# Expert weights of a mixture-of-experts layer read from one array in order of use, instead of from three arrays in their own order

## The chip, the cores and the metric

One core of one Trainium2 chip runs the whole program. The metric is the device time of one execution in microseconds (us). Before the change the median of three runs is 1352.35 us, with 1351.14 us the lowest and 1352.84 us the highest.

## What is computed

One layer of an encoder on 512 tokens of width 1024, all in float32. Three blocks, each followed by a residual sum and a layer norm:

```python
x = layer_norm(a * x + hybrid_mixer(x, ...))             # 8 heads of windowed attention beside a gated conv
x = layer_norm(a * x + memory_cross_attention(x, mem))   # 4 heads over 256 memory tokens
x = layer_norm(a * x + expert_choice_moe(x, ...))        # 16 experts

def expert_choice_moe(x, w_router, w_gate, w_up, w_down):
    affinity = softmax(x @ w_router)                     # (512, 16)
    gates, idx = top_k(affinity.T, 64)                   # each expert picks 64 tokens
    xe = x[idx]                                          # 16 x 64 x 1024
    hid = silu(xe @ w_gate) * (xe @ w_up)                # 16 x 64 x 2048
    ye = (hid @ w_down) * gates
    return scatter_add(idx, ye)
```

The arrays of the experts are `w_exp_gate` and `w_exp_up` (16 x 1024 x 2048) and `w_exp_down` (16 x 2048 x 1024), 8 MB for each expert and array, 384 MB together. Each weight is used once, so that each has to be read once from DRAM.

## The kernel before

**Stages.** The mixer and the cross attention fill the first 375 us. Then come the experts, two at a time: 8 pairs, the first written out and the other seven in a loop (`Fori(1, PAIRS)`) on each engine. A pair gathers the picked tokens with matmuls against a 0/1 matrix (line 929), does gate and up (line 970), turns the hidden activations (line 979), does down (line 992) and adds the result to the output tokens (matmul of line 1002, sum of line 1265). After the last pair comes the last layer norm, with the stores of the output.

**Chunks.** The weights of an expert come in 12 chunks (`CPE`) of 2 MB, those of a pair in 24 (`CPP`): for each half of the columns of gate and up, four chunks in the order gate, up, gate, up; then four of down. A chunk is [128 partitions, 4, 1024] float32 in SBUF: 16 KB in each partition, without gaps. In the chunk, partition p and index k hold the 4 KB run of row 128 (k0 + k) + p of the weight matrix. So a chunk is 512 runs of 4 KB in DRAM. For gate and up a row is 8 KB long and the run is one half of it; for down a row is 4 KB long, and the 512 runs of a chunk lie one behind the other, in an order other than that of the partitions. `exp_src(pair, j)` gives the DRAM side of chunk j, `exp_chunk(j, first)` the SBUF side.

**The ring.** SBUF has 8 slots of one chunk each. In the first pair two further chunks (8 and 9) go to other places, chunk 9 in five small transfers (line 378). All the loads are issued by SyncE (SP), in the order of use: `load_exp` has a wait of its own ahead of it, on the semaphore `exp_used`, which TensorE raises behind the last matmul of each chunk. Chunk j is issued when chunk j - 8 is used. The last chunk of each pair is loaded in two halves of 1 MB (line 335), all others in one transfer (line 338). TensorE waits in `expert_in` for the chunk's own semaphore. Nothing but the weights' loads goes through SP's queue during the experts; ScalarE's queue has small loads of the earlier stages.

**The matmuls of a chunk.** The code has 8 matmuls for a chunk, 4 k by 2 halves of the 1024 columns, each with 64 tokens loaded into the array and [128, 512] of the chunk streamed through it. In the trace they are 16 instructions in float32.

Of the kernel before, what the change touches and what calls it, by code (L numbers as in the profile page):

```python
# [1 line left out]

# [10 lines left out]
P = 128  # L36
D, S, M = 1024, 512, 256
# [6 lines left out]
E, CAP, FF = 16, 64, 2048  # L44
# [4 lines left out]
SLOT = 4096  # L49
# [4 lines left out]
CPE = 12  # L54
CPP = 2 * CPE
# [66 lines left out]


def build(nc, x, mem, w_in, na_rpb, conv_w, w_mix_out, ln1_g, ln1_b, w_mem_q, w_mem_k, w_mem_v, w_mem_out,
          ln2_g, ln2_b, w_router, w_gate, w_up, w_down, ln3_g, ln3_b, consts, out):
    with ExitStack() as ctx:
        def sb(name, *shape):
            return ctx.enter_context(nc.sbuf_tensor(name, [P, *shape], F32))
# [60 lines left out]
        gate = kv[:, 64:128].rearrange("p (i t e) -> p i t e", i=PAIRS, t=TT)  # L189
# [112 lines left out]
                return scattered[k][2][:, 512 * c:512 * c + 512] if k < 3 else scattered[3 + c][2]  # L302
            return exp_chunk(j, first)[:, k, 512 * c:512 * c + 512]

        wg_v = w_gate[0].rearrange("e (k p) f -> e p k f", p=P)
        wu_v = w_up[0].rearrange("e (k p) f -> e p k f", p=P)
        wd_v = w_down[0].rearrange("e (k p) d -> e p k d", p=P)

        def exp_src(pair, j):
            e, n = 2 * pair + j // CPE, j % CPE  # L310
            if n < 8:
                g, w, k = n // 4, (wg_v, wu_v)[n % 2], 4 * (n % 4 // 2)
                return w[bass.ds(e, 1), :, k:k + 4, 1024 * g:1024 * g + 1024].rearrange("e p k f -> (e p) k f")
            k = 4 * (n - 8)
            return wd_v[bass.ds(e, 1), :, k:k + 4, :].rearrange("e p k d -> (e p) k d")

        def key_tokens(v, a):

# [8 lines left out]
        def _(sp):  # L327
# [3 lines left out]
            def load_exp(j, pair=0, first=True):  # L331
                landed = extra_in[0] if first and j == EXTRA else exp_in[exp_slot(j, first)]
                if j == CPP - 1:
                    for h, semaphore in enumerate((half_in, landed)):
                        sp.dma_start(exp_chunk(j, first)[:, 2 * h:2 * h + 2], exp_src(pair, j)[:, 2 * h:2 * h + 2])\
                            .then_inc(semaphore, 16)
                    return
                sp.dma_start(exp_chunk(j, first), exp_src(pair, j)).then_inc(landed, 16)  # L338
# [38 lines left out]
            for row, cols, room in scattered:  # L377
                sp.dma_start(room, exp_src(0, EXTRA + 1)[:, row, cols]).then_inc(extra_in[1], 16)
# [910 lines left out]


_INS = ["x", "mem", "w_in", "na_rpb", "conv_w", "w_mix_out", "ln1_g", "ln1_b", "w_mem_q", "w_mem_k", "w_mem_v",
        "w_mem_out", "ln2_g", "ln2_b", "w_router", "w_exp_gate", "w_exp_up", "w_exp_down", "ln3_g", "ln3_b"]


# [19 lines left out]
```

## Time and profile before

| | |
|---|---|
| span of the profiled execution | 1350.2 us |
| median of three runs (no profile) | 1352.35 us |
| from the start to the first expert matmul of line 929 | 375.7 us |
| TensorE (PE) busy | 1165.1 us, 86% |
| DMA from 394 to 1321 us | 409 GB/s |
| read from DRAM | 435.50 MB |

The profiled execution has no time of its own apart from its span; the span runs from its first to its last instruction and is 2.15 us below the median of the runs (1352.35 - 1350.2), which is what lies around it. The page divides the span into 40 slices of 33.75 us each; a digit is a busy share in tenths. A DMA packet is one run of bytes that one of the 16 DMA engines moves. A mean DMA share can come out a little over 1, because an engine's packets overlap at their ends.

### The profile page before, as it was taken

Reading aid. Unit: us, or ns where it says so; the run is one execution under the profiler, and the core shown is the slowest. Engines: PE = TensorE matmul, PEld = TensorE weight load, DVE = VectorE, ACT = ScalarE, POOL = GpSimd, SP = SyncE. Lnnn points to the kernel's source line nnn. Section 1 sums busy time; section 2 is a strip of 40 time slices with the busy share of each in tenths; the row PEclk is TensorE's granted clock in tenths of the full one; section 3 lists DMA queues with packets and bytes.
Section 4 is the critical chain, followed back from the end, with each engine's and each line's share of the span. In section 5 each row is a group of like instructions: output and inputs, shape, how many; then the busy total and the mean of one; then the engine's idle time right before and its main releaser. Section 6 shows DMA issues by size and latency. Waiting matters only on the chain.

```text
span 1350.2 us, 13739 instructions
## 1 busy us (share of the span) xinstructions
PE 1165.1 (86%) x5680; PEld 591.3 (44%) x5680; DVE 291.4 (22%) x472; ACT 196.5 (15%) x366; POOL 123.0 (9%) x60
## 2 busy tenths in 40 slices
PE   7999988999599999889779978987897799789874
PEld 6786866897553343243224322422432243234221
DVE  2014587646610020020002002000200020020005
ACT  4233434043100000000000001000000000010003
POOL 3312323430003000000000000000000000000003
PEclk9999999999689999999999999999999999999997
DMA  9513112065759999999999999999999999999993
GB/s 317 129 63 125 63 63 94 0 235 233 280 196 409 409 409 410 409 409 410 410 410 410 410 409 410 409 410 410 410 410 410 410 410 410 410 410 410 410 410 121
DMA packets 123228, 438.03 MB, mean 324 GB/s; under 512 B 6575, under 2 KB 11966, under 8 KB 123198
## 3 DMA queue, kind: packets, MB, share of 16 engines
q1 hardware_dynamic: 118080, 432.09, 81.0%
q10 hardware_dynamic: 5118, 5.52, 1.6%
q8 instruction: 22, 0.36, 0.1%
q14 instruction: 8, 0.07, 0.0%
HBM read 435.50 MB, written 2.11 MB: 324 GB/s over the span
## 4 chain that ended last, share of the span: by engine, by line
PE 53%; DMA 31%; DVE 7%; SPq 3%; ACT 3%; issue 1%; POOL 1%; POOLq 0%; ACTq 0%; DVEq 0%
PE bank L970 17%; DMA ring<-in_w_exp_down 13%; DMA ring<-in_w_exp_up 11%; PE bank L992 8%; DMA ring<-in_w_exp_gate 7%; PE bank L929 5%; PE bank L1002 4%; SPq L338 3%; PE bank L693 3%; PE bank L698 3%; PE bank L695 3%; PE bank L682 2%; PE bank L674 1%; PE bank L804 1%; PE bank L806 1%
## 5 line engine op out<-in xcount | busy, mean ns | idle before, releaser
L970 PE MATMUL bank<-ring,yt 128*64 128x512 f32 x2048 | 454.6, 596 | 69.8 <-DMA ring<-in_w_exp_up 35.5
L970 PEld LDWEIGHTS bank<-ring,yt 128*64 128x64 f32 x2048 | 143.7, 137 | 363.5 <-issue 259.1
L992 PE MATMUL bank<-ring,yt 128*64 128x512 f32 x992 | 222.6, 596 | 38.1 <-DMA ring<-in_w_exp_down 25.9
L992 PEld LDWEIGHTS bank<-ring,yt 128*64 128x64 f32 x992 | 71.9, 137 | 168.9 <-issue 115.5
L1259 DVE TENSOR_TENSOR work<-bank,work 128x512 f32<-128x512 f32 x32 | 22.1, 692 | 473.9 <-PE bank L970 473.9
L641 ACT ACTIVATE work<-bank 128x512 f32<-128x512 f32 x32 | 19.1, 597 | 576.5 <-PE bank L970 576.5
L409 POOL TENSOR_SCALAR stat<-stat 128x1 f32<-128x1 f32 x3 | 1.7, 554 | 906.2 <-ACT work L659 906.2
L1265 DVE TENSOR_TENSOR xT<-bank,xT 128x512 f32<-128x512 f32 x64 | 44.3, 691 | 171.6 <-PE bank L1002 171.6
L929 PE MATMUL bank<-yt,res 128*128 128x128 f32 x512 | 63.4, 284 | 13.3 <-DVE yt L1245 13.3
L929 PEld LDWEIGHTS bank<-yt,res 128*128 128x128 f32 x512 | 60.4, 197 | 25.6 <-DVE xT L1265 17.7
L402 POOL TENSOR_TENSOR piece<-ring,piece 128x1024 fp32r<-128x1024 f32 x24 | 57.7, 2406 | 146.3 <-ACT piece L477 146.3
L1002 PE MATMUL bank<-yt 128*128 128x512 f32 x128 | 61.7, 618 | 6.0 <-ACT yt L648 6.0
L693 PE MATMUL bank<-x_hi,piece 128*128 128x512 f32 x192 | 49.2, 398 | 3.6 <-ACT piece L477 1.9
L644 ACT ACTIVATE yt<-bank 128x512 f32<-128x512 f32 x32 | 19.1, 597 | 203.8 <-PE bank L979 203.8
L695 PE MATMUL bank<-x_lo,piece 128*128 128x512 f32 x192 | 47.5, 389 | 0.0
L698 PE MATMUL bank<-x_hi,piece 128*128 128x512 f32 x192 | 47.5, 389 | 0.0
L1002 PEld LDWEIGHTS bank<-yt 128*128 128x128 f32 x128 | 19.7, 188 | 48.4 <-DVE xT L1265 31.6
L693 PEld LDWEIGHTS bank<-x_hi,piece 128*128 128x128 f32 x192 | 35.0, 188 | 11.0 <-ACT ring L503 2.2
L695 PEld LDWEIGHTS bank<-x_lo,piece 128*128 128x128 f32 x192 | 36.1, 188 | 7.6
L698 PEld LDWEIGHTS bank<-x_hi,piece 128*128 128x128 f32 x192 | 36.0, 188 | 7.5
L648 ACT ACTIVATE yt<-bank 64x512 f32<-64x512 f32 x32 | 18.9, 591 | 121.9 <-PE bank L992 121.5
L674 PE MATMUL bank<-cst,work 128*128 128x128 f32 (+1 forms) x100 | 15.4, 277 | 23.1 <-DVE work L1222 13.2
(147 smaller groups left out, 960.2 us busy)
## 6 DMA issues: line engine op xcount, KB each, us to landing
ring<-in_w_exp_gate SPq DMA_DIRECT2D x64, 2048.0 KB, 23.6
ring<-in_w_exp_up SPq DMA_DIRECT2D x64, 2048.0 KB, 23.7
ring<-in_w_exp_down SPq DMA_DIRECT2D x54, 2048.0 KB, 23.8
ring<-in_w_exp_down SPq DMA_DIRECT2D x16, 1024.0 KB, 19.9
ring<-in_w_in SPq DMA_DIRECT2D x5, 2048.0 KB, 9.0
ring<-in_w_mix_out SPq DMA_DIRECT2D x2, 2048.0 KB, 7.7
res<-in_x SPq DMA_DIRECT2D x4, 512.0 KB, 5.5
ring<-in_w_in SPq DMA_DIRECT2D x4, 512.0 KB, 9.1
```

Source lines behind the costliest of these rows:

```text
L338: sp.dma_start(exp_chunk(j, first), exp_src(pair, j)).then_inc(landed, 16)
L402: nc.gpsimd.tensor_tensor(piece[:, p % 2, 1, :, :], raw_piece(p), piece[:, p % 2, 0, :, :].bitcast(F32), ALU.subtract).then_inc(lo_split, 1)
L674: mm = nc.tensor.transpose(pt[n % 2][0:cols, a * P:a * P + rows], src, ident[0:rows, 0:rows])
L682: mm = nc.tensor.matmul(pj[n % 2][:, 0:width], lhs(c), rhs(c), start=c == 0, stop=c == k - 1)
L693: nc.tensor.matmul(pj[n % 2][:, :], hi[:, k, :], x_hi[:, k, :], start=k == 0, stop=False)
L695: nc.tensor.matmul(pj[n % 2][:, :], hi[:, k, :], x_lo[:, k, :], start=False, stop=False)
L698: mm = nc.tensor.matmul(pj[n % 2][:, :], lo[:, k, :], x_hi[:, k, :], start=False, stop=k == KT - 1)
L929: mm = nc.tensor.matmul(pv[k // 4][:, P * (k % 4):P * (k % 4) + P], res[:, t, P * k:P * k + P], pick[:, t].rearrange("p e n -> p (e n)"), ...
L970: mm = nc.tensor.matmul(bank[2 * g + n % 2][64 * c:64 * c + 64, :], xeT[:, kk, 64 * e:64 * e + 64], exp_rhs(j, first, k, c), start=kk == 0 ...
L992: mm = nc.tensor.matmul(bank[5][64 * n:64 * n + 64, :], hidT[:, s, 64 * c:64 * c + 64], exp_rhs(j, first, s, n), start=(g, c, s) == (0, 0, ...
L1002: mm = nc.tensor.matmul(pv[(c + 1) % 2][:, :], scat[:, t, :], ye[:, 512 * n:512 * n + 512], start=True, stop=True)
L1265: nc.vector.tensor_tensor(y, pv[(c + 1) % 2][:, :], y, ALU.add).then_inc(mix_kept, 1)
```

## The change

The host makes one array `w_exp` of the three, of 192 chunks x 128 partitions x 4096 floats (`SLOT`), in order of use. Partition p of a chunk is then 16 KB in one piece, and the chunk 2 MB in one piece. The DRAM side of a load is one line. SBUF side, slots, order, waits, sizes and counts of transfers, and all matmuls stay; so do the two halves of the last chunk (each partition's 8 KB are in one piece in it) and the five small transfers of chunk 9 (4 KB or 2 KB in each partition, as before).

```diff
-        wg_v = w_gate[0].rearrange("e (k p) f -> e p k f", p=P)
-        wu_v = w_up[0].rearrange("e (k p) f -> e p k f", p=P)
-        wd_v = w_down[0].rearrange("e (k p) d -> e p k d", p=P)
+        chunks = experts.rearrange("c p (k n) -> c p k n", k=4)
 
         def exp_src(pair, j):
-            e, n = 2 * pair + j // CPE, j % CPE
-            if n < 8:
-                g, w, k = n // 4, (wg_v, wu_v)[n % 2], 4 * (n % 4 // 2)
-                return w[bass.ds(e, 1), :, k:k + 4, 1024 * g:1024 * g + 1024].rearrange("e p k f -> (e p) k f")
-            k = 4 * (n - 8)
-            return wd_v[bass.ds(e, 1), :, k:k + 4, :].rearrange("e p k d -> (e p) k d")
+            return chunks[bass.ds(CPP * pair + j, 1)].rearrange("c p k n -> (c p) k n")
...
+def expert_chunks(gate, up, down):
+    out = np.empty((E, CPE, P, 4, 1024), np.float32)
+    for n in range(8):
+        w = (gate, up)[n % 2][0].reshape(E, 2, 4, P, 2, 1024)
+        out[:, n] = w[:, n % 4 // 2, :, :, n // 4].transpose(0, 2, 1, 3)
+    out[:, 8:] = down[0].reshape(E, 4, 4, P, D).transpose(0, 1, 3, 2, 4)
+    return out.reshape(E * CPE, P, SLOT)
```

## Rows read from the trace of the kernel before

**Rows 1.** The page: busy tenths of TensorE and DMA, GB/s, in 40 slices.

```profile
PE   7999988999599999889779978987897799789874
...
DMA  9513112065759999999999999999999999999993
GB/s 317 129 63 125 63 63 94 0 235 233 280 196 409 409 409 410 409 409 410 410 410 410 410 409 410 409 410 410 410 410 410 410 410 410 410 410 410 410 410 121
```

**Rows 2.** The chain that ended last, two pairs' parts: start us, us, what.

```profile
679.12 24.28 DMA ring<-in_w_exp_down
...
703.53 7.10 PE bank L992 x32
...
751.04 24.03 DMA ring<-in_w_exp_gate
...
777.03 20.48 DMA ring<-in_w_exp_up
797.51 28.76 DMA ring<-in_w_exp_down
826.41 7.10 PE bank L992 x32
```

**Rows 3.** The same view: start of the first pair and of the second.

```profile
375.71 6.76 PE bank L929 x40
...
484.87 4.73 PE bank L929 x40
```

**Rows 4.** DMA view, 394 to 1321 us: packets, queues, loads with us to landing.

```profile
DMA packets 95629, 379.45 MB, mean 409 GB/s; under 512 B 3016, under 2 KB 3016, under 8 KB 95621
q1 hardware_dynamic: 95621, 379.32, 102.5%
ring<-in_w_exp_gate SPq DMA_DIRECT2D x60, 2048.0 KB, 23.6
ring<-in_w_exp_down SPq DMA_DIRECT2D x52, 2048.0 KB, 23.8
```

**Rows 5.** Timeline, last pair: start us, us, instructions, [idle before <-releaser].

```profile
1292.24 3.65 PE L970 MATMUL bank<-ring,yt 128*64 128x512 f32 x16 [1.38 <-DMA ring<-in_w_exp_up]
1297.35 3.65 PE L970 MATMUL bank<-ring,yt 128*64 128x512 f32 x16 [1.46 <-DMA ring<-in_w_exp_gate]
1302.47 3.65 PE L970 MATMUL bank<-ring,yt 128*64 128x512 f32 x16 [1.47 <-DMA ring<-in_w_exp_up]
1307.68 3.65 PE L992 MATMUL bank<-ring,yt 128*64 128x512 f32 x16 [0.97 <-DMA ring<-in_w_exp_down]
1312.72 3.65 PE L992 MATMUL bank<-ring,yt 128*64 128x512 f32 x16 [1.38 <-DMA ring<-in_w_exp_down]
1317.92 7.09 PE L992 MATMUL bank<-ring,yt 128*64 128x512 f32 x32 [0.97 <-DMA ring<-in_w_exp_down]
```

**Rows 6.** Stretches: us, busy us by engine, granted clock, DMA share, GB/s.

```profile
80.00:83.00 3.00, 3.00 (x15) 2.49 (x14) 0.00 (x0) 0.00 (x0) 0.00 (x0) 1.00 1.05 403
303.00:308.00 5.00, 4.10 (x29) 3.63 (x27) 2.21 (x8) 3.30 (x12) 0.00 (x0) 1.00 1.02 417
344.00:348.00 4.00, 3.51 (x26) 3.40 (x25) 2.59 (x3) 1.08 (x2) 1.52 (x1) 0.73 1.03 425
600.00:1300.00 700.00, 594.43 (x2782) 223.06 (x2782) 62.95 (x91) 46.28 (x72) 0.00 (x0) 1.00 1.03 410
```

**Rows 7.** DMA view of 8 to 16 us, and of 79 to 83 us.

```profile
DMA packets 4282, 2.46 MB, mean 308 GB/s; under 512 B 78, under 2 KB 4160, under 8 KB 4282
...
DMA packets 781, 1.60 MB, mean 400 GB/s; under 512 B 0, under 2 KB 0, under 8 KB 781
```

**Rows 8.** Loads issued by SP, 394 to 1321 us: min/median/max ns, first and last start.

```profile
L338 SPq DMA_DIRECT2D ring<-in_w_exp_gate x60: 367/4700/10248, 396.0 to 1268.5; - x60
L338 SPq DMA_DIRECT2D ring<-in_w_exp_up x60: 368/4783/10250, 399.4 to 1279.0; - x60
```

**Rows 9.** The page: the instruction queue, and packets of the whole span by size.

```profile
DMA packets 123228, 438.03 MB, mean 324 GB/s; under 512 B 6575, under 2 KB 11966, under 8 KB 123198
q8 instruction: 22, 0.36, 0.1%
```

More of the change, by code:

```diff
@@ L124, in build @@
 def build(nc, x, mem, w_in, na_rpb, conv_w, w_mix_out, ln1_g, ln1_b, w_mem_q, w_mem_k, w_mem_v, w_mem_out,
-          ln2_g, ln2_b, w_router, w_gate, w_up, w_down, ln3_g, ln3_b, consts, out):
+          ln2_g, ln2_b, w_router, experts, ln3_g, ln3_b, consts, out):
     with ExitStack() as ctx:
@@ L1291 @@
 _INS = ["x", "mem", "w_in", "na_rpb", "conv_w", "w_mix_out", "ln1_g", "ln1_b", "w_mem_q", "w_mem_k", "w_mem_v",
-        "w_mem_out", "ln2_g", "ln2_b", "w_router", "w_exp_gate", "w_exp_up", "w_exp_down", "ln3_g", "ln3_b"]
+        "w_mem_out", "ln2_g", "ln2_b", "w_router", "w_exp", "ln3_g", "ln3_b"]
+def expert_chunks(gate, up, down):
[5 more added lines that the diff above has]
+    return out.reshape(E * CPE, P, SLOT)
 def kernel(**inputs):
@@ L1300 @@
     arrays, args = {}, []
+    laid = {
+        "w_exp": expert_chunks(*(np.asarray(inputs[f"w_exp_{w}"]) for w in ("gate", "up", "down"))),
+    }
     for name in _INS:
-        a = inputs[name]
+        a = laid[name] if name in laid else inputs[name]
         if name == "na_rpb":
```

## The prediction, made before the changed kernel was built or run

> **What bounds the kernel now.** I read the page's slices first. From slice 13 on (about 394 us) the DMA digit is 9 and the rate is 409 or 410 GB/s in every slice up to the last, while PE moves between 7 and 9 [rows 1]. One resource is flat at its top, the other breathes: the reader is to see in this that the transfers, and not TensorE, pace the experts. The DMA view of 394 to 1321 us says the same in one line: 379.32 MB on SP's queue, 102.5% of the 16 engines' time [rows 4]. At 2.097 MB a chunk that is 379.32 / 2.097 = 181 chunks without a gap.
>
> The chain of waits confirms it. In a pair it runs through landings of 20 to 29 us, and the same matmul group of line 992 starts at 703.53 and at 826.41 us, 122.88 us apart [rows 2]. A pair has 24 chunks, so a chunk takes 122.88 / 24 = 5.120 us. The first pair, whose chunks were there in time, took 484.87 - 375.71 = 109.16 us [rows 3]. So TensorE alone would need 13.7 us a pair less than the DMA gives it. In the timeline of the last pair TensorE starts a chunk, works 3.65 us, and idles about 1.4 us for the next one [rows 5].
>
> **The change, part by part.**
>
> *TensorE, VectorE, ScalarE, POOL.* No instruction is added, removed or moved: 0 us.
>
> *SP.* The same number of loads behind the same waits. The address of a load is worked out from one index instead of two; SP is not idle-bound here: its loads take 4.7 us in the median and 0.37 us at the least [rows 8]. An instruction that can be done in 0.37 us and takes 4.7 is held up by a full queue. Its cost does not reach the end as long as a load is issued before the engines run dry, and a load lands 23.6 us after its issue where 5.12 us would be its own share [rows 4], so at least four chunks are ahead of it. If that cover were gone, each load would cost its 0.37 us beside the 5.12, still nothing. I take 0 for SP. If packets become four times larger, SP's queue holds more bytes, its loads drop towards 0.4 us, and SP waits for a free slot instead; the landing then counts up to 8 chunks, 8 x 5.12 = 41 us. That is another place of the same wait.
>
> *First ten chunks and chunk 9's five pieces.* They land before the experts begin. The first pair ran 109.16 us without a chain piece of a DMA [rows 3], so nothing of them is on the path: 0 us.
>
> *The 181 chunks behind them.* Here every 0.1 us of a chunk counts 181 times: 18.1 us. Two things change for a chunk, the place of its bytes in DRAM and the size of a packet.
>
> The place. In the timeline TensorE starts gate and up chunks at 1292.24, 1297.35 and 1302.47 us, 5.11 and 5.12 apart, and down chunks at 1307.68, 1312.72 and 1317.92, 5.04 and 5.20 apart [rows 5]. But the two kinds lie differently: a chunk of gate or up is 512 runs of 4 KB with gaps of 4 KB, a chunk of down is already 2 MB without a gap. Had DRAM been slowed by the gaps, down would be quicker; it is not. Their time from issue to landing is equal too, 23.6 and 23.8 us [rows 4]. So what the change does to the place is worth 0 by the nearest rows. Its bounds: the third kind of layout is new in that neighbouring partitions lie 16 KB apart, and no row shows it.
>
> The size of a packet. Now 95,621 packets carry 379.32 MB, none of them over 8 KB [rows 4]; taking off the 3,016 small ones leaves 92,605 of 4,096 bytes. If there is a fixed cost for each packet beside its bytes, a 16 KB packet pays it once instead of four times. What do rows say of it? 2 KB packets ran at 403 GB/s in a stretch of 3 us, and at 400 in one of 4 us [rows 6, 7]. That is 2048 x 16 / 400 = 81.9 ns a packet and engine. 4 KB packets take 4096 x 16 / 410 = 159.8 ns in the long stretch [rows 6]. A fixed part is then 2 x 81.9 - 159.8 = 4.0 ns. A 16 KB packet would take 4 x 159.8 - 3 x 4.0 = 627 ns, 418 GB/s, and a chunk 5.02 us. In short stretches, with the queue just filled, 4 KB packets ran at 417 and 425 GB/s [rows 6], 157.2 and 154.2 ns; by these the fixed part is 6.6 or 9.6 ns and a 16 KB packet takes 609 or 588 ns, 430 or 446 GB/s.
>
> But the short stretches say more than that. The same 4 KB packets, of the same weights, run at 417 to 425 GB/s for the first 4 or 5 us and then at 409 to 410 for 900 us. The engines can therefore take a 4 KB packet faster than they do. What holds the long stretch at 410 is something that they share or that stands ahead of them, and it shows no sign of a price by the packet. Writing the packets' descriptors is not it either: from 8 to 16 us 4,282 packets, nearly all under 2 KB, went through in 8 us, 1.9 ns each, where the long stretch needs one every 10 ns [rows 7]. A limit in bytes does not see the packet's size. I take the value for a limit in bytes, 0 us for a chunk, because the long stretch itself is the row nearest to the changed kernel, and keep as ends -44 us (430 GB/s: 2.097 / 0.430 = 4.877 us instead of 5.12 for a chunk, times 181) and, the other way, the slower rival's +22 us below. The 446 GB/s would be 4.70 us a chunk and -76 us; it rests on a stretch of 4 us and is the far end.
>
> The sum against the profiled execution: span 1350.2 + 0 = 1350.2 us, and with the 2.15 us around it 1352.35. I forecast 1352 us, no change.
>
> Here a page of the skill speaks for a gain. The Trainium skill, "DMA: Bandwidth & Descriptors", section "Why small descriptors are slow (HBM only)", gives the engine a fixed cost of about 3 cycles for each packet, beside one cycle for 32 bytes. By that a 16 KB packet needs 515 cycles where four of 4 KB need 524; a chunk would fall by 1.7%, as an estimate from that page to 5.03 us, and the kernel by 16 us. The trace's 2 KB stretch agrees in size with such a cost (4.0 ns); that it is what binds the long stretch, the short stretches at 417 and 425 speak against.
>
> The same page's table "Specifications" wants at least 512 bytes in a transfer for the full line rate. By that rule 4 KB runs are well past the point from which size matters, and the change is worth nothing. No row here shows more than 8 KB from DRAM into SBUF.
>
> **The rivals.**
>
> *A. The packet has a price and it binds (faster).* For it: 2 KB packets are slower for their bytes than 4 KB ones, 400 against 410. Against it: the 417 to 425 stretches. It decides as soon as a chunk lands in less than 5.12 us, because TensorE has 13.7 us a pair to give, down to 109.16 / 24 = 4.55 us a chunk. Its time: with 4.0 ns, 5.018 us a chunk, 181 x -0.102 = -18.5 us, 1334 us; with the rate of the first 5 us kept for good (417 GB/s, 5.029 us) much the same, 1336 us; with 6.6 ns, 1308 us. I take 1332 us as its middle.
>
> *B. The new places in DRAM are read more slowly (slower).* One mechanism: all the partitions of a chunk now start 16 KB apart and each engine reads 16 KB from one place before it goes on, so that the engines read in step from places that may share a part of the memory. The place is the reading side of the 181 chunks; it decides as soon as a chunk takes more than 5.12 us, since there is no slack on the DMA side at all. Price from the nearest row that ran slower at full queue, the 2 KB stretch at 400 GB/s: 2.097 / 0.400 = 5.243 us, 181 x 0.123 = +22 us, 1374 us. For it: of the 30 packets over 8 KB in the trace 22 are instruction loads of 16 KB (0.36 MB / 22), and they took 0.1% of 16 engines' span [rows 9], 0.001 x 16 x 1350.2 / 22 = 0.98 us each, 17 GB/s for an engine instead of 25.6. Those go to another memory than SBUF; at their rate a chunk would take 7.8 us and the kernel 490 us more, which I name as the far end and do not believe. Against it: gate, up and down are two different layouts with one and the same 5.12 us.
>
> *C. The change doesn't do what it says.* The queue could still cut the 16 KB into packets of 4 KB. Then only the place changes, and the time stays at 1352 us. The changed profile would tell C from my forecast, the time would not.
>
> **How the numbers follow.** No change by a limit in bytes 0.40 and C 0.16, both 1352 us, together 0.56; A 0.34; B 0.10. About 0.2% (2.7 us) is what a measurement of this kernel can tell from no change. So faster 0.34, within 0.2% 0.56, slower 0.10. The forecast is that of the likeliest case, 1352 us. For 8 in 10 the range takes in the no-change cases and most of A, down to 1318 us, which leaves out the part of A with 6.6 ns (some 0.08), and ends at 1357 us above, which leaves out B (0.09).
>
> **What would show it.** Right: the slices keep 409 or 410 GB/s from 394 us on, the group of line 992 repeats every 122.88 us, and TensorE's idle ahead of a chunk stays near 1.4 us. That packets grew: about 23,000 of them over 8 KB in place of 92,605 of 4 KB, SP's loads near 0.4 us instead of 4.7, and landings of up to 41 us. In that case with 410 GB/s unchanged, my limit in bytes is shown. Packets grown and the rate at 418 or more is A; I would have erred in taking the short stretches for proof that the packet's cost is covered. A rate under 409 with larger packets, or with packets of 4 KB at new places, is B. Unchanged packets with unchanged time are C. What would make it wrong apart from these is a stage before 375 us that moves, and nothing of the change reaches it.

## The result, and the profile after

The changed kernel takes 1313.88 us (median of 4 runs, 1311.94 to 1314.76), the kernel before 1351.78 us beside it: a ratio of 0.9716, with a 95% interval of 0.9704 to 0.9729. That is 37.9 us less, where the forecast was no change and the range ended at 1318 us. The span of the profiled execution is 1311.9 us against 1350.2.

The page's slices for DMA and GB/s, to be read against [rows 1], and its line on packets, against the one in [rows 9] (a slice is now 32.8 us):

```profile
DMA  9513112047549999999999999999999999999992
GB/s 318 140 65 129 64 65 97 1 193 288 195 157 409 425 427 427 428 428 429 428 429 426 430 428 427 429 428 429 426 430 429 427 429 428 429 426 430 430 425 109
DMA packets 50908, 438.03 MB, mean 334 GB/s; under 512 B 6575, under 2 KB 11966, under 8 KB 25406
```

The same megabytes go in 50,908 packets instead of 123,228. 25,502 of them (50,908 - 25,406) are of 8 KB or more, where there were 30. The rate has gone from 409 or 410 to between 425 and 430 GB/s in every slice from 426 us on, nearly as flat as it was. So the packets did grow, and the rate did not stay.

SP's loads from 394 to 1285 us (min/median/max ns), against [rows 8], and the median us from issue to landing in the DMA view, against [rows 4]:

```profile
L308 SPq DMA_DIRECT2D ring<-in_w_exp x172: 327/333/348, 396.9 to 1244.3; - x172
```

```profile
ring<-in_w_exp SPq DMA_DIRECT2D x172, 2048.0 KB, 30.3
```

A load takes SP 0.33 us where it took 4.7, and lands 30 us after its issue where it took 23.6: SP is no longer held up by a full queue, and waits for free slots instead. This came as forecast, and it is not where the time comes from (see the experiment with two loads in flight, below).

The chain of waits, where [rows 2] and [rows 3] had landings at every turn (start us, us, what):

```profile
376.30 7.05 PE bank L899 x40
...
709.15 4.73 PE bank L899 x40
713.88 3.62 PE bank L940 x16
...
720.38 24.18 PE bank L940 x112
...
745.84 7.09 PE bank L962 x32
...
754.27 7.09 PE bank L962 x32
...
761.95 7.06 PE bank L940 x32
...
769.16 35.28 DMA ring<-in_w_exp
...
804.49 3.65 PE bank L962 x16
...
826.75 4.73 PE bank L899 x40
...
944.29 4.73 PE bank L899 x40
...
1061.87 4.73 PE bank L899 x40
...
1179.39 4.73 PE bank L899 x40
```

(Lines 899, 940, 962 and 972 are lines 929, 970, 992 and 1002 of the kernel before; a chunk is 16 instructions.) In the pair that starts at 709.15 us TensorE goes through 14 chunks at its own pace (16 + 112 + 32 + 32 + 32 instructions) and meets the DMA at the 15th: its timeline has the first wait for a landing before 770.23 us. The last ten chunks still come at the pace of the DMA. From 826.75 to 1179.39 us three pairs take 352.64 us, 117.55 us a pair, 4.898 us a chunk, against 122.88 and 5.120. The DMA remains the bound, with 8.4 us a pair to go to the 109.16 us of [rows 3].

The timeline of the last pair has the same step, 4.80 to 4.99 us from chunk to chunk, where [rows 5] had 5.04 to 5.21:

```profile
1245.31 3.65 PE L940 MATMUL bank<-ring,yt 128*64 128x512 f32 x16 [1.24 <-DMA ring<-in_w_exp]
1250.30 3.65 PE L940 MATMUL bank<-ring,yt 128*64 128x512 f32 x16 [1.34 <-DMA ring<-in_w_exp]
1255.10 3.65 PE L940 MATMUL bank<-ring,yt 128*64 128x512 f32 x16 [1.15 <-DMA ring<-in_w_exp]
1260.00 3.65 PE L940 MATMUL bank<-ring,yt 128*64 128x512 f32 x16 [1.25 <-DMA ring<-in_w_exp]
```

**Where the 38.3 us of the spans are.** The experts begin 0.6 us later (376.30 against 375.71). From the start of pair 0 to the start of pair 7 it is 803.1 us against 836.6 (1179.39 - 376.30; 1212.31 - 375.71), 33.5 less. The start of pair 7 in the chain of the kernel before:

```profile
1212.31 4.73 PE bank L929 x40
```

From there to the end it is 132.5 against 137.9, 5.4 less. 33.5 + 5.4 - 0.6 = 38.3. By chunks: 181 x (5.120 - 4.898) = 40.2 us. Of the 1.9 us between the two, 0.6 are the later start; the slice from 394 to 426 us, at 409 GB/s instead of 428, accounts for some 32.8 x 19 / 428 = 1.5. Why that slice is slower was not followed up.

### The profile page after: what moved, and what is told of

Same layout as the page of the kernel before. It is cut to its first block, busy times and chain, and to the rows that moved or that the text cites. A ratio compares the mean times of both kernels' runs of the same rounds, so it can differ in the third digit from the quotient of the medians.

```text
span 1311.9 us, 13711 instructions
## 1 busy us (share of the span) xinstructions
PE 1162.6 (89%) x5680; PEld 593.1 (45%) x5680; DVE 291.4 (22%) x472; ACT 196.1 (15%) x366; POOL 123.6 (9%) x60
## 2 busy tenths in 40 slices
DMA packets 50908, 438.03 MB, mean 334 GB/s; under 512 B 6575, under 2 KB 11966, under 8 KB 25406
## 4 chain that ended last, share of the span: by engine, by line
PE 71%; DMA 16%; DVE 6%; ACT 3%; issue 1%; POOL 1%; POOLq 0%; SPq 0%; DVEq 0%; ACTq 0%
PE bank L940 24%; DMA ring<-in_w_exp 16%; PE bank L962 16%; PE bank L899 5%; PE bank L972 4%; PE bank L663 3%; PE bank L668 3%; PE bank L665 3%; PE bank L652 2%; PE bank L644 1%; ACT yt L614 1%; PE bank L949 1%; PE bank L725 1%; PE bank L774 1%; PE bank L776 1%
```

## The experiments

Two theories stood after the result. **Packet**: each packet costs an engine a fixed time beside its bytes, and the four times fewer packets are the whole gain. **Place**: the bytes now lie in DRAM in the order of use, and the packets' size doesn't matter. The kernel before and the changed one give the packet theory its two numbers: 32 packets and 5.120 us, 8 packets and 4.899 us a chunk and engine, so (5.120 - 4.899) / 24 = 9.2 ns a packet and 4.825 us for the bytes. (4.899 is 117.58 / 24, the pair as the expectations took it.) All later expectations use them unchanged.

**Runs of 4 KB at the new places.** All three kernels with gaps differ from the changed one by this, with `RUN` of 1024, 2048 and 512 floats and `GAP` of 64 floats (256 bytes); the SBUF side is the same memory, viewed as runs.

```diff
-        chunks = experts.rearrange("c p (k n) -> c p k n", k=4)
+        chunks = experts.rearrange("c p (m r) -> c p m r", r=RUN + GAP)
 
         def exp_src(pair, j):
-            return chunks[bass.ds(CPP * pair + j, 1)].rearrange("c p k n -> (c p) k n")
+            return chunks[bass.ds(CPP * pair + j, 1), :, :, 0:RUN].rearrange("c p m r -> (c p) m r")
```

> The host's layout of the changed kernel, but with 256 bytes of gap behind each 4 KB run: a partition's chunk is 4 runs within 17 KB, so the places are those of the changed kernel to within 2% while a packet can't be longer than 4 KB. Theory 'packet': what counts is the number of packets. The kernel before took 122.88 / 24 = 5.120 us a chunk with 32 packets of 4 KB on each of 16 engines, the changed one 117.58 / 24 = 4.899 us with 8 packets of 16 KB; so a packet costs (5.120 - 4.899) / 24 = 9.2 ns beside its bytes and the bytes cost 4.825 us. Here: 5.120 us a chunk, 1352 us. Rival 'place': the order of the bytes in DRAM counts, packets don't: 4.90 us a chunk, 1314 us.

1353.38 us, a ratio to the kernel before of 1.0002 (0.9992 to 1.0012). Two pairs begin at

```profile
968.30 4.73 PE bank L911 x40
1091.18 4.73 PE bank L911 x40
```

122.88 us apart. That is the 122.88 us of the kernel before. With packets of 4 KB and the bytes at their new places the whole gain is gone. (The gaps make a partition's 16 KB into 17 KB, 6% and not the 2% that the expectation names.) The 4 KB runs lie 4 KB apart in gate and up before, without gaps in down before, and 256 bytes apart here; a chunk takes 5.120 us on the average of a pair in both kernels. Place falls.

**Runs of 16 KB, scattered.**

```diff
-        chunks = experts.rearrange("c p (k n) -> c p k n", k=4)
+        chunks = experts.rearrange("p (c n) -> c p n", n=SLOT + GAP)[:, :, 0:SLOT].rearrange("c p (k n) -> c p k n", k=4)
```

> The opposite: packets of 16 KB, but in DRAM each partition has a row of its own with its 192 pieces of 16 KB (256 bytes of gap behind each), so that the 128 pieces of a chunk lie 3 MB apart. Theory 'packet': 8 packets an engine, 4.90 us a chunk, 1314 us. Rival 'place': the 2 MB in one piece were what helped; scattered they take at least the 5.12 us of the kernel before, 1352 us or more.

1313.0 us, 0.9704 (0.9687 to 0.972). The stretch from 600 to 1250 us of this kernel (us, busy us by engine, granted clock, DMA share, GB/s):

```profile
600.00:1250.00 650.00, 576.47 (x2704) 216.05 (x2700) 61.63 (x90) 46.28 (x72) 0.00 (x0) 1.00 1.01 428
```

The 128 pieces of a chunk are 3 MB apart and it costs nothing. That a chunk is 2 MB in one piece has no part in the gain.

**Runs of 8 KB and of 2 KB.**

> The changed kernel with runs of 8 KB (256 bytes of gap behind each). Theory 'packet' at 9.2 ns: 4.825 + 16 x 0.0092 = 4.972 us a chunk, 181 x 0.073 = 13 us over the changed kernel, 1327 us. Rival 'place': 1314 us. A threshold between 4 and 16 KB instead of a price by the packet would give 1314 or 1352 us.

1326.2 us, 0.9808 (0.9791 to 0.9824).

```profile
950.11 4.73 PE bank L911 x40
1069.42 4.73 PE bank L911 x40
```

119.31 us a pair, 4.971 us a chunk; 4.972 was expected. There is no threshold between 4 and 16 KB.

> The changed kernel with runs of 2 KB (256 bytes of gap behind each), a long stretch of 2 KB packets, which the kernel before doesn't have. Theory 'packet' at 9.2 ns: 4.825 + 64 x 0.0092 = 5.414 us a chunk, 181 x 0.515 = 93 us over the changed kernel, 1407 us. By the rate of 400 GB/s that 2 KB packets had in a stretch of 4 us of the kernel before: 5.243 us a chunk, 1376 us. By a limit in bytes of 410 GB/s: 5.12 us, 1352 us.

1406.11 us, 1.0401 (1.0384 to 1.0419). The DMA view of this kernel from 600 to 1250 us:

```profile
DMA packets 124778, 251.46 MB, mean 387 GB/s; under 512 B 1999, under 2 KB 1999, under 8 KB 124778
```

251.46 MB in 650 us are 386.9 GB/s and 5.42 us a chunk; 5.414 was expected. This is the long stretch of 2 KB packets that the kernel before lacked: 387 GB/s, and not the 400 to 403 that the prediction read from stretches of 3 and 4 us.

**Down's weights alone.** `w_exp_down` is laid out by the host as 16 KB a partition; gate and up are read as before.

```diff
-        wd_v = w_down[0].rearrange("e (k p) d -> e p k d", p=P)
+        wd_v = w_down.rearrange("e c p (k d) -> e c p k d", k=4)
...
-            k = 4 * (n - 8)
-            return wd_v[bass.ds(e, 1), :, k:k + 4, :].rearrange("e p k d -> (e p) k d")
+            return wd_v[bass.ds(e, 1), n - 8].rearrange("e p k d -> (e p) k d")
```

> One part of the change alone: only the down weights are laid out by the host (16 KB a partition in one piece); gate and up are read as in the kernel before. A chunk of down was 2 MB without a gap before as well, so that only the packets' size and the order within the 2 MB change. Theory 'packet': 8 of 24 chunks fall from 5.120 to 4.899 us, 181 / 3 x 0.221 = 13 us: 1339 us, 121.1 us a pair. Rival 'place' as the gaps of gate and up: nothing, 1352 us.

1340.24 us, 0.9909 (0.9896 to 0.9923).

```profile
838.72 4.73 PE bank L928 x40
...
1202.17 4.73 PE bank L928 x40
```

Three pairs in 363.45 us, 121.15 a pair; (16 x 5.120 + 8 x 4.899) comes to 121.11. A chunk of down was one gapless piece of 2 MB before, so only the size of its packets and the order within the 2 MB have changed, and the kernel with scattered pieces shows that the order costs nothing. The packets' size explains this third of the gain.

**At most two loads in flight.** Ahead of each load, from chunk 12 on, SP also waits until the load two places earlier has landed. The loop over the pairs is written out on SP, so that the waits are constants; `DEPTH` is 2.

```diff
+            def landed_by(n):
+                if n >= EXTRA + EXTRAS:
+                    sp.wait_ge(exp_in[exp_slot(n % CPP, False)], 16 * ((n - EXTRA - EXTRAS) // SLOTS + 2))
...
+            for i in range(1, PAIRS):
                 for j in range(CPP):
                     sp.wait_ge(exp_used, i * CPP + (j - SLOTS + 1))
+                    landed_by(i * CPP + j - DEPTH)
                     load_exp(j, i, first=False)
```

> The kernel before, with one more wait ahead of each load of the experts from chunk 12 on: the load two places earlier has landed, so that at most two loads are in flight (4.6 on average before). SP's loop over the pairs is written out for it. It asks why 4 KB packets ran at 417 to 425 GB/s in short stretches and at 410 for 900 us. Theory 'depth': a full queue adds some 5 ns to each packet; with two in flight a chunk takes 2.097 / 0.420 = 4.99 us, 181 x 0.13 = 23 us less, 1329 us. Rival 'start-up': the short stretches are high because packets counted in them began before, or because engines are out of step only later; then depth is nothing: 5.12 us a chunk, 1352 us. If two loads are too few to keep the engines busy: over 1352 us, with gaps in the DMA's share.

1353.19 us, 1.0008 (0.9998 to 1.0018).

> The same extra wait in the changed kernel. Theory 'depth': 8 packets of 16 KB save some 5 ns each, 4.86 us instead of 4.90, 181 x 0.04 = 7 us less, 1307 us. Rival 'start-up': 1314 us.

1313.83 us, 0.972 (0.9704 to 0.9736). That there were only two in flight is seen in the DMA view of the first of the two, 600 to 1250 us, where a load lands 10.2 us after its issue, twice 5.1:

```profile
DMA packets 67077, 266.14 MB, mean 409 GB/s; under 512 B 2106, under 2 KB 2106, under 8 KB 67075
...
ring<-in_w_exp_gate SPq DMA_DIRECT2D x42, 2048.0 KB, 10.2
```

SP's loads fell to 0.37 us in it, as they did with the change, and not a us was gained. The full queue was a sign of the small packets and no cost.

**Two queues.** The odd chunks of pairs 1 to 7 are issued by GpSimd, with semaphores of their own; the first kernel has 4 KB packets (the kernel before), the second 16 KB.

```diff
-                for j in range(CPP):
+                for j in range(0, CPP, 2):
                     sp.wait_ge(exp_used, i * CPP + (j - SLOTS + 1))
                     load_exp(j, i, first=False)
...
+                    for i in range(1, PAIRS):
+                        for j in range(1, CPP, 2):
+                            pool.wait_ge(exp_used, i * CPP + (j - SLOTS + 1))
+                            landed = pool_in[exp_slot(j, False) // 2]
+                            room, src = exp_chunk(j, False), exp_src(i, j)
...
+                                nc.gpsimd.dma_start(room, src).then_inc(landed, 16)
```

> The kernel before (4 KB packets), with the odd chunks of pairs 1 to 7 issued by GpSimd instead of SP, so that each engine has two queues to take packets from. Theory 'ring': the 9.2 ns lie between two packets of one queue and the other queue's packet fills them; then a chunk falls from 5.12 towards 4.83 us and the kernel by up to 45 us, to about 1305. Theory 'engine': the price is the engine's own for each packet; 5.12 us a chunk, 1352 us. GpSimd makes its packets in software; if it makes them slower than one load in 10.2 us it becomes the bound, over 1352 us.

1355.34 us, 1.0026 (1.0017 to 1.0036). The DMA view, 600 to 1250 us:

```profile
DMA packets 67107, 266.25 MB, mean 410 GB/s; under 512 B 2107, under 2 KB 2107, under 8 KB 67107
...
q1 hardware_dynamic: 33551, 133.26, 51.4%
q0 software_dynamic: 33556, 132.99, 51.1%
```

Each queue has half of the packets and the rate is the same 410 GB/s. One queue's packets don't fill the time between the other's. (The kernel is 3.6 us slower than the one before beside it, which its rate doesn't show; where that arises was not followed up.)

This leaves one rival: the price could be charged by something that all 16 engines share. The packet records of the kept traces (start, duration and bytes of each packet) speak to that. Where at most 8 packets are under way at a time, as at the end of a load, a packet takes 84 ns at 2 KB (150 packets) and 159 ns at 4 KB (52 packets) in the kernel before, 309 ns at 8 KB (42 packets, the kernel with 8 KB runs) and 611 ns at 16 KB (6 packets, the changed kernel); all are medians. From 600 to 1250 us, with all engines at work and one size in each kernel, they take 88, 164, 314 and 613 ns. Twice a 2 KB packet less a 4 KB packet is 2 x 84 - 159 = 9 ns, and 2 x 159 - 309 is 9 ns again. So the fixed part is there while half of the engines or more stand idle: it is each engine's own.

> The same split over two queues in the changed kernel (16 KB packets). Theory 'ring': 4.83 instead of 4.90 us a chunk, 160 x 0.07 = 11 us less, 1303 us. Theory 'engine': 1314 us.

1321.17 us, 0.9775 (0.976 to 0.979), 8.6 us over the changed kernel beside it (1312.61). The rate is 428 GB/s in most of it, with dips such as 391 from 960 to 980 us; before that one TensorE waited 4.45 us for a landing inside a chunk, and the matmul that adds the results to the tokens (line 989 of this kernel) then took 9.51 us instead of 7.7, in a stretch with a granted clock of 0.74, which is partly the lower of its two levels:

```profile
920.00:940.00 20.00, 15.66 (x74) 4.96 (x70) 0.69 (x1) 1.19 (x2) 1.07 (x2) 1.00 1.01 427
940.00:960.00 20.00, 14.83 (x38) 5.69 (x39) 6.92 (x10) 2.46 (x3) 0.54 (x1) 0.74 1.01 428
960.00:980.00 20.00, 20.00 (x118) 10.38 (x118) 1.38 (x2) 0.60 (x1) 0.54 (x1) 1.00 0.97 391
```

Which of the two, TensorE's slower turn or the order in which two queues bring chunks, makes up the 8.6 us was not tried. Both theories were about the rate, and the rate says "engine".

**Packets of 32 KB.** Two neighbouring chunks in one load of 4 MB; the host puts a partition's two pieces together.

```diff
+        def exp_part(pair, at, n):
+            part = experts[bass.ds(pair, 1), at * P * SLOT:(at + n) * P * SLOT]
+            return part.rearrange("c (p n) -> (c p) n", p=P)
...
+                s = exp_slot(j, first)
+                sp.dma_start(ring[:, s * SLOT:(s + 2) * SLOT], exp_part(pair, j, 2)).then_inc(landed, 16)
```

> One step further than the change: from chunk 10 of the first pair on, two neighbouring chunks come in one load of 4 MB into two neighbouring slots, with 32 KB of each partition in one piece; chunk 0 of a pair and its last chunk stay alone. Of 24 chunks of a pair 22 then take 4 packets of 32 KB on each engine. Theory 'packet' at 9.2 ns: such a chunk takes 4.825 + 4 x 0.0092 = 4.862 us instead of 4.899, some 166 x 0.037 = 6 us less. On the other side the first chunk of a load is there one chunk later, which costs up to 4.9 us once, behind the last double load, where the DMA sets the end. Together 1308 to 1313 us. Rival: packets are never over 16 KB, then 1314 us or, with the later landing, up to 1319.

1315.91 us, 0.9733 (0.972 to 0.9746). Two stretches of it:

```profile
394.00:500.00 106.00, 100.86 (x482) 38.40 (x478) 11.76 (x17) 8.43 (x13) 10.71 (x2) 1.00 0.98 414
600.00:1250.00 650.00, 585.09 (x2740) 219.43 (x2740) 62.28 (x90) 46.32 (x72) 0.00 (x0) 0.99 1.00 431
```

and two of its pairs:

```profile
949.17 4.73 PE bank L916 x40
1065.91 4.73 PE bank L916 x40
```

116.74 us a pair, where 22 chunks of 4.862 and 2 of 4.899 make 116.76. The price by the packet holds to 32 KB. The kernel is slower nonetheless than the changed one beside it (1312.61 us) and than the 1308 to 1313 us expected. The loss lies in the first two pairs: a load of 4 MB waits for two free slots and the DMA engines run out of work (their share is 0.87 from 394 to 410 us), so that the third pair starts at 599.01 us, 6.7 us behind the changed kernel beside it. The later landing behind the last double load, which the expectation names, isn't seen: from the start of the last pair to the end it is 131.8 us against 132.5.

**Packets of 32 KB in 14 of 24 chunks.**

> 32 KB packets again, where they cost no lead: in pairs 1 to 7 the chunks 1 and 2, 3 and 4, 5 and 6, 9 to 16 come two by two in loads of 4 MB; 0, 7, 8 and 17 to 23 stay alone, so that a free slot is used across the turn of a pair and the last chunks land one by one. Theory 'packet' at 9.2 ns: 14 of 24 chunks take 4.862 instead of 4.899 us, 7 x 14 x 0.037 = 3.6 us less than the changed kernel: 1310 us, and 428 GB/s or a little more in every slice from 394 us on, without the 414 GB/s that the kernel with nearly all loads doubled had up to 500 us. If the loss of that kernel came from the 4 MB loads themselves, and not from the lead, it comes back here: 1314 us or more.

1312.29 us, 0.9703 (0.969 to 0.9716). The changed kernel beside it:

> The changed kernel beside the other two, for a comparison on one chip: 1314 us by every theory.

1312.66 us, 0.9706 (0.9693 to 0.972). The changed kernel beside the two with two queues and the first with 32 KB:

> The changed kernel itself, beside the other three on the same chip: 1314 us by every theory.

1312.61 us, 0.9703 (0.9689 to 0.9716).

So the gain of 3.6 us that was expected of the kernel with some packets of 32 KB is not there. Its stretches:

```profile
394.00:500.00 106.00, 100.86 (x482) 38.51 (x480) 11.76 (x17) 8.43 (x13) 10.71 (x2) 1.00 1.01 428
500.00:600.00 100.00, 93.83 (x438) 34.70 (x436) 11.07 (x16) 8.43 (x13) 0.00 (x0) 1.00 0.98 418
600.00:1250.00 650.00, 578.09 (x2696) 215.74 (x2694) 61.57 (x89) 46.31 (x72) 0.00 (x0) 0.99 1.00 430
```

The first 106 us are mended, but between 500 and 520 us the DMA engines run out of work once (a share of 0.88): 418 GB/s for 427 in the changed kernel is (427 - 418) x 100 / 428 = 2.1 us of transfer lost. The price itself holds: the four pairs from 709.35 to 1177.43 us take 117.02 us each, against 117.56 in the changed kernel beside it, where 14 x 0.037 = 0.52 us less was expected. The span is 1309.5 us and that of the changed kernel beside it 1311.1, which the runs can't tell apart. No version that measurably beats the changed kernel was found.

The price over all sizes, from the long stretches (expected values from 4 and 16 KB alone):

| packet | GB/s, 600 to 1250 us | us a chunk | expected |
|---|---|---|---|
| 2 KB | 387 | 5.42 | 5.414 |
| 4 KB | 410 | 5.120 | (given) |
| 8 KB | 422 | 4.971 | 4.972 |
| 16 KB | 428 | 4.898 | (given) |
| 32 KB, 22 chunks of 24 | 431 | 4.864 | 4.865 |

## Why the prediction was wrong

*The bound.* Right: the transfers pace the experts, 181 chunks follow one another without a gap, and each 0.1 us of a chunk is 18 us. The measured 0.222 us a chunk gave 38 us.

*TensorE, SP, the first ten chunks at 0.* Right. The start of the experts moved by 0.6 us. SP's loads and landings moved as described (0.33 us and 30 us), and the kernels with two loads in flight show that this is worth nothing either way.

*The place of the bytes at 0.* Right, and for the right reason: down's chunks were gapless and no quicker. The kernel with 4 KB runs at the new places and the one with pieces 3 MB apart show it. Rival B's slower reading did not appear.

*The size of a packet at 0.* This is the step that failed: "What holds the long stretch at 410 is something that they share or that stands ahead of them, and it shows no sign of a price by the packet." The rows showed that 4 KB packets can go at 417 to 425 GB/s for 4 or 5 us. From that followed only that the long stretch is slower than a short one. The prediction made of it that the long stretch's limit counts bytes, and that step had no row. The long stretch had packets of one size alone, so a limit in bytes and a limit in packets fit it equally well. The runs put in its place: in the long stretch a packet costs an engine 9.2 ns beside its bytes, from 2 to 32 KB, and each engine pays it by itself. The trace of the kernel before already held this, in the 84 and 159 ns that a packet of 2 KB and one of 4 KB took with few under way; the prediction went by rates alone.

*The size in rival A.* A named the right mechanism and sized it at 4.0 ns, 1334 us, because it set 2 KB packets of a stretch of 4 us against 4 KB packets of a stretch of 700 us. Compared in like stretches (387 and 410 GB/s), the same formula gives 2 x 2048 x 16 / 387 - 4096 x 16 / 410 = 169.3 - 159.8 = 9.5 ns. Two short stretches set side by side, 400 and 417, give 2 x 81.9 - 157.2 = 6.6 ns, 1308 us; the text had this number and left it out of the range. The low end of 1318 us cut off just the sizes of A that hold. That the size of 6.6 ns comes to 430 GB/s and -44 us, near the measured 428 and -38, is luck: a packet of 157.2 ns for the 160 of the long stretch makes it too fast, and 6.6 ns for 9.2 makes the gain of larger packets too small.

The Trainium skill, "DMA: Bandwidth & Descriptors", section "Why small descriptors are slow (HBM only)", had the mechanism that the runs show, a fixed cost for each packet, which it puts at about 3 cycles. The prediction's estimate from it was 16 us; the measured gain is 38. The sign agrees; the measured price is more than twice as large. The rule of at least 512 bytes for the full line rate, from "Specifications" on the same page, does not hold here as a rule of no loss above that: 4 KB is 4% under 16 KB, and 2 KB 10%.

*Rival C.* The packets did grow; it falls with the page's line on packets.

*Open.* Why a 4 KB packet runs faster in the first 5 us of a burst than later. In the packet records it is the packet's own time: 159 ns in the median from 303 to 308 and from 344 to 348 us, 164 ns from 600 to 1250 us. Two loads in flight and two queues left the long stretch at 409 and 410 GB/s, so neither the number of loads in flight nor the one queue accounts for it.

## What to carry to other kernels

When a kernel is bound by transfers, count packets as well as bytes: here an engine needed 4.825 us for its 128 KB of a chunk and 9.2 ns for each packet, and a layout by the host that makes 16 KB runs out of 4 KB ones gave 2.8% of the time. When one resource runs flat with one kind of work, its rate alone does not say whether it counts bytes or pieces; another size in the same long stretch does, and a short stretch is no stand-in. Packets of 32 KB won another 0.037 us a chunk here, but their loads of 4 MB need two free slots at once, and the kernels with them came out 3.3 us slower and no faster (1315.91 and 1312.29 us, against 1312.61 and 1312.66).

## What was not expected of the hardware

One load gave packets of the full contiguous run, up to 32 KB, without being asked to: the kernel with 4 MB loads moves 280.40 MB in 11,069 packets from 600 to 1250 us, 1,232 of them under 512 bytes. Where the 16 KB runs of a chunk lie in DRAM made no difference between one piece of 2 MB and 128 pieces 3 MB apart (1313.88 and 1313.0 us). Splitting the loads over two queues left the rate at 410 GB/s, each with half of the packets. And the fixed part of a packet stands in its own duration even with few packets under way: 84 ns for 2 KB and 159 ns for 4 KB in the kernel before.
